# A block of seventeen residual stages in one kernel: the gated linear attention (Hgrn) stage between its projection products, cross attention in pairs of heads, and a finer wait before the down projections

## The reference

```
def gla_chunk(q, k, v, log_f, chunk):
    gc = jnp.cumsum(blocks(log_f), axis=3)
    g_last = gc[:, :, :, -1]
    q_dec = q * jnp.exp(gc)
    k_inv = k * jnp.exp(-gc)
    k_end = k * jnp.exp(g_last[:, :, :, None] - gc)
    att = jnp.where(causal, jnp.einsum('bnhlk,bnhsk->bnhls', q_dec, k_inv), 0.0)
    o_intra = jnp.einsum('bnhls,bnhsv->bnhlv', att, v)
    def step(state, inp):
        qd, ke, vv, gl = inp
        o = jnp.einsum('bhlk,bhkv->bhlv', qd, state)
        state = state * jnp.exp(gl)[..., None] + jnp.einsum('bhsk,bhsv->bhkv', ke, vv)
        return state, o
...
def hgrn2_mixer(h, in_w, lower_bound, norm_w, out_w):
    q, f, i, g = jnp.split(h @ in_w, 4, axis=-1)
    forget = lb + (1.0 - lb) * jax.nn.sigmoid(f.astype(jnp.float32))
    o = gla_chunk(heads(jax.nn.silu(q)) * H_EXPAND ** -0.5, heads(1.0 - forget), heads(i),
                  heads(jnp.log(forget)), HGRN_CHUNK)
    o = rmsnorm_2(o.astype(h.dtype), norm_w) * jax.nn.silu(heads(g))
    return o.reshape(bsz, seq, D_MODEL) @ out_w
...
def memory_cross_attention(h, mem_n, wq, wkv, wo):
    s = jnp.einsum('blhd,bmhd->bhlm', q, k).astype(jnp.float32) * X_HEAD_DIM ** -0.5
    p = jax.nn.softmax(s, axis=-1).astype(h.dtype)
    o = jnp.einsum('bhlm,bmhd->blhd', p, v).reshape(bsz, seq, D_MODEL)
    return o @ wo
```

## Time and profile before

| | us |
|---|---|
| median of 3 runs | 4009.58 |
| lowest and highest run | 3997.74, 4010.38 |
| the profiled execution | 4006.53 |
| span of its instructions | 4004.8 |
| TensorE matmul busy | 3823.6 |
| VectorE busy | 1061.4 |
| ScalarE busy | 721.6 |
| mean granted TensorE clock | 0.982 of full speed |

### The profile page before, as it was taken

The page is one execution under the profiler, slowest core; times in us unless marked ns, Lnnn a source line. Parts: engine busy times, 40 slices in busy tenths (PEclk is TensorE's granted clock), DMA queues, the critical chain, the costliest instruction groups (busy, mean ns, idle before and its releaser), DMA issues.

```text
span 4004.8 us, 37903 instructions
## 1 busy us (share of the span) xinstructions
PE 3823.6 (95%) x16756; PEld 2747.2 (69%) x16756; DVE 1061.4 (27%) x2069; ACT 721.6 (18%) x1361; POOL 16.4 (0%) x43
## 2 busy tenths in 40 slices
PE   6999999999999999999995899999999999999998
PEld 5856785875587775778564568667666877757684
DVE  5434341502410243112103202126420212431120
ACT  1004200001510242111001111023221102521110
POOL 1000000000000000000000000000000000000000
PEclk9999999999999999999996899999899999999999
DMA  9752584744234423334440124332222434333342
GB/s 374 283 199 107 212 300 176 276 147 147 107 145 154 153 106 126 131 130 160 147 147 21 65 105 168 141 135 103 106 107 105 153 142 154 119 121 132 132 154 88
DMA packets 42451, 598.45 MB, mean 149 GB/s; under 512 B 4736, under 2 KB 4752, under 8 KB 6192
## 3 DMA queue, kind: packets, MB, share of 16 engines
q1 hardware_dynamic: 41024, 589.94, 40.0%
q0 software_dynamic: 1264, 6.10, 0.4%
HBM read 594.97 MB, written 1.05 MB: 149 GB/s over the span
## 4 chain that ended last, share of the span: by engine, by line
PE 92%; DVE 5%; ACT 2%; issue 1%; DMA 0%; DVEq 0%
PE ps L449 33%; PE ps L328 12%; PE ps L345 9%; PE ps L1906 4%; PE ps L2202 3%; PE ps L361 3%; PE ps L2221 3%; PE ps L1939 2%; PE ps L1414 2%; PE ps L1064 1%; PE ps L1409 1%; PE ps L1434 1%; PE ps L474 1%; PE ps L645 1%; PE ps L371 1%
## 5 line engine op out<-in xcount | busy, mean ns | idle before, releaser
L449 PE MATMUL ps<-hT,ring 128*128 128x256 f32 (+1 forms) x7360 | 1327.7, 343 | 3.6 <-DVE stat L309 3.6
L449 PEld LDWEIGHTS ps<-hT,ring 128*128 128x128 f32 x7360 | 1194.9, 191 | 134.2 <-issue 7.7
L328 PE MATMUL ps<-ring,aT 128*128 128x512 f32 x1088 | 477.4, 600 | 20.1 <-DVE aT L2326 14.5
L328 PEld LDWEIGHTS ps<-ring,aT 128*128 128x128 f32 x1088 | 208.2, 193 | 280.2 <-issue 257.3
L345 PE MATMUL ps<-ring,aT 128*128 128x512 f32 x848 | 371.1, 595 | 9.0 <-ACT aT L2266 7.8
L345 PEld LDWEIGHTS ps<-ring,aT 128*128 128x128 f32 x848 | 160.1, 191 | 205.4 <-issue 194.4
L208 DVE SCALAR_TENSOR_TENSOR memT<-big,silu_c,memT 128x512 f32<-128x512 f32 x238 | 179.0, 752 | 8.5
L1906 PE MATMUL ps<-hT,ring 128*128 128x256 f32 x768 | 173.1, 382 | 0.0
L383 ACT ACTIVATE big<-x 128x1024 f32<-128x1024 f32 x34 | 35.9, 1057 | 759.5 <-DVE x L426 432.5
L1906 PEld LDWEIGHTS ps<-hT,ring 128*128 128x128 f32 x768 | 145.5, 191 | 26.1 <-issue 7.7
L426 DVE TENSOR_TENSOR x<-x,ps 128x1024 f32<-128x1024 f32 x22 | 26.9, 1221 | 432.1 <-PE ps L345 432.1
(11 more groups left out here) (481 smaller groups left out, 3450.0 us busy)
## 6 DMA issues: line engine op xcount, KB each, us to landing
ring<-weights_in SPq DMA_DIRECT2D x244, 2048.0 KB, 7.7
big<-ada_in SPq DMA_DIRECT2D x34, 2048.0 KB, 7.7
ring<-ada_in SPq DMA_DIRECT2D x2, 2048.0 KB, 27.4
big<-b_gate_in POOLq DMA_DIRECT2D x1, 1536.0 KB, 15.1
x<-x_in SPq DMA_DIRECT2D x1, 1024.0 KB, 5.0
big<-b_gate_in POOLq DMA_DIRECT2D x1, 1024.0 KB, 9.0
big<-mem_in POOLq DMA_DIRECT2D x1, 1024.0 KB, 5.3
out<-big SPq DMA_DIRECT2D x2, 512.0 KB, 2.6
```

The source lines that it names most:

```text
L328: last = pe.matmul(ps[:, 2 * t + half, :], aT[:, 4 * j + k, t * P:(t + 1) * P], w[:, k, half * 512:(half + 1) * 512], start=(4 * j + k == ...
L449: last = pe.matmul(ps[:, bank + m // 2, (m % 2) * SEQ + at:(m % 2) * SEQ + at + n], w[:, k, m * P:(m + 1) * P], hT[:, k, at:at + n], start ...
```

## The change

1. **Hgrn.** The pieces now come in the order f, f, q, i, q, i, g, g. The mixer works in two halves of four heads. Its products are no longer behind the last piece but at 48 numbered slots between the products of the last six pieces (`hgrn_fill_pe`). The intra-chunk products are full 128x128 products, 8 for a half (`hgrn_inside_pe`), where each chunk had its own; the states start from the first update and there are 7 updates and 7 state products for a half. The last half's transposes are inside the down projection (`down_halves_pe`, which is the former `down_attn_pe` with its waits and its transpose function as arguments). The making of the keys is moved to a function of its own (`down_keys_pe`). The constants of the scan go to `gdn_work`.
2. **Cross attention.** Scores, softmax, transposes and products are made for two pairs of heads. The second pair's scores and both pairs' transposes are between the products of v. The down projection waits for the first pair's tiles only, and for the second pair's before its second piece.
3. **Down projections of the gated stages.** `down_pe` and `last_pe` wait at first for the tenth piece's tiles, and for the eleventh's (`then`) ahead of their own last piece.

```
+        def hgrn_inside_pe(pe, half):
+            pe.wait_ge(hgrn_dve_done, HGRN_DVE[f"masked{half}"])
+            pe.wait_ge(hgrn_act_done, HGRN_ACT[f"v{half}"])
+            for t in range(TT):
+                for h in range(4):
+                    last = pe.matmul(ps[:, t, h * P:(h + 1) * P], hgrn_scores(half)[:, h, t, :], hgrn_tokens(6144, half)[:, t, h * P:(h + 1) * P], start=(h == 0), stop=False, skip_group_check=True)
+        def hgrn_update_pe(pe, half, c):
+            t, j = c // 4, c % 4
+            if c >= 2:
+                pe.wait_ge(hgrn_dve_done, HGRN_DVE[f"state{half}{c - 1}"])
+            for h in range(4):
+                at = 512 * half + h * P
+                last = pe.matmul(ps[:, 2 + c % 2, h * P:(h + 1) * P], view(big, 14336, TT, D)[32 * j:32 * j + 32, t, at:at + P],
+                                 view(big, 6144, TT, D)[32 * j:32 * j + 32, t, at:at + P], start=True, stop=True)
+        def hgrn_inter_pe(pe, half, c):
+            t, j = c // 4, c % 4
+            pe.wait_ge(hgrn_dve_done, HGRN_DVE[f"state{half}{c}"])
+            for h in range(4):
+                last = pe.matmul(ps[32 * j:32 * j + 32, t, h * P:(h + 1) * P], hgrn_part(0, half)[:, h, 32 * c:32 * c + 32], hgrn_state(c)[:, h, :], start=False, stop=True, skip_group_check=True)
+        def hgrn_fill_pe(pe, slot):
+            if slot == 8:
+                hgrn_ends_pe(pe, 0)
+            if slot == 11:
+                hgrn_scores_pe(pe, 0)
+            if slot == 13:
+                hgrn_ends_pe(pe, 1)
+            if slot == 27:
+                hgrn_scores_pe(pe, 1)
+            for half in range(2):
+                c = slot - 17 - 16 * half
+                if c == 0:
+                    hgrn_inside_pe(pe, half)
+                if 0 <= c < 7:
+                    hgrn_update_pe(pe, half, c)
+                if 0 < c < 8:
+                    hgrn_inter_pe(pe, half, c)
+            if slot == 45:
+                hgrn_turn_pe(pe, 0)
+        def hgrn_pe(pe, i, c0):
             first_channels_pe(pe, i, c0)
+            freed = ("f0", "f1", "q0", "v0", "q1", "v1")
+            for c in range(6):
+                pe.wait_ge(hgrn_act_done, HGRN_ACT[freed[c]])
...
+                            if k % 4 == 0:
+                                hgrn_fill_pe(pe, 8 * c + 2 * m + k // 4)
...
+                            if k % 2 == 0:
+                                hgrn_fill_pe(pe, 8 * c + 4 * t + k // 2)
...
+        def hgrn_act(act, c0):
+            act.wait_ge(hgrn_dve_done, HGRN_DVE["shifted"])
             act.activation(small[:, 8:40], small[:, 8:40], ACT.Exp).then_inc(hgrn_act_done, 1)
+            hgrn_chunk_act(act, c0, 0, hgrn_part(2048, 0), ACT.Sigmoid)
+            hgrn_chunk_act(act, c0, 1, hgrn_part(2048, 1), ACT.Sigmoid)
+            for half in range(2):
+                act.wait_ge(hgrn_dve_done, HGRN_DVE[f"forget{half}"])
+                act.activation(hgrn_flat(12288, half), hgrn_flat(2048, half), ACT.Ln).then_inc(hgrn_act_done, 1)
+            for half in range(2):
+                act.wait_ge(hgrn_dve_done, HGRN_DVE[f"sum{half}"])
+                act.activation(hgrn_flat(12288, half), hgrn_flat(10240, half), ACT.Exp).then_inc(hgrn_act_done, 1)
+
+                act.wait_ge(hgrn_dve_done, HGRN_DVE[f"gap{half}"])
+                act.activation(hgrn_flat(14336, half), hgrn_flat(14336, half), ACT.Exp).then_inc(hgrn_act_done, 1)
+                act.activation(hgrn_flat(8192, half), hgrn_flat(10240, half), ACT.Exp, scale=-1.0).then_inc(hgrn_act_done, 1)
+            hgrn_chunk_act(act, c0, 2, hgrn_part(0, 0), ACT.Silu)
+            for half in range(2):
+                act.wait_ge(hgrn_pe_done, HGRN_PE[f"ends{half}"])
+                act.wait_ge(hgrn_dve_done, HGRN_DVE["end1"])
+                act.copy(hgrn_tokens(14336, half), ps[:, 0:2, :]).then_inc(hgrn_act_done, 1)
+            hgrn_chunk_act(act, c0, 3, hgrn_tokens(6144, 0), ACT.Copy)
+            hgrn_chunk_act(act, c0, 4, hgrn_part(0, 1), ACT.Silu)
+            hgrn_out_act(act, 0)
+            hgrn_chunk_act(act, c0, 5, hgrn_tokens(6144, 1), ACT.Copy)
+            hgrn_root_act(act, 0)
...
+            hgrn_query_dve(dve, 0)
+            hgrn_masked_dve(dve, 0)
+            hgrn_states_dve(dve, 0, 1, 8)
+            hgrn_query_dve(dve, 1)
+            hgrn_masked_dve(dve, 1)
+            hgrn_norm_dve(dve, 0)
+            hgrn_states_dve(dve, 1, 1, 8)
+            hgrn_gate_dve(dve, 0)
+            hgrn_tiles_dve(dve, 0)
+            hgrn_norm_dve(dve, 1)
+            hgrn_gate_dve(dve, 1)
+            hgrn_tiles_dve(dve, 1)
```

Cross attention and the waits:

```
+            xattn_scores_pe(pe, n, 0)
+            for j in range(2):
+                pe.wait_ge(xattn_act_done, 8 * n + j + 1)
+                w = arrived(pe, c0 + 2 + j).rearrange("p (k c) -> p k c", k=KT)
                 for t in range(TT):
+                    if (j, t) == (0, 1):
+                        xattn_scores_pe(pe, n, 1)
+                    if (j, t) == (1, 1):
+                        xattn_turn_pe(pe, n, 0)
                     for k in range(KT):
+                        if (j, t, k) == (1, 1, 4):
+                            xattn_turn_pe(pe, n, 1)
...
+            xattn_values_pe(pe, n, 0)
+            xattn_values_pe(pe, n, 1)
...
             for t in range(TT):
                 for c in range(nc - 2, nc):
+                    if then and (t, c) == (0, nc - 1):
+                        pe.wait_ge(*then)
...
-            down_pe(pe, 0, (swiglu_dve_done, 11), c0=11, nk=22, ada=range(14, 18))
+            down_pe(pe, 0, (swiglu_dve_done, 10), c0=11, nk=22, ada=range(14, 18), then=(swiglu_dve_done, 11))
...
-            down_pe(pe, 7, (xattn_act_done, 7), c0=108, nk=8)
+            down_pe(pe, 7, (xattn_act_done, 8), c0=108, nk=8, then=(xattn_dve_done, 10))
...
-            down_pe(pe, 8, (convglu_dve_done, 44), c0=121, nk=22)
-            hgrn_pe(pe, 0, 8, c0=127)
-            down_pe(pe, 9, (hgrn_dve_done, 34), c0=135, nk=8, kc0=137, ki=1)
+            down_pe(pe, 8, (convglu_dve_done, 40), c0=121, nk=22, then=(convglu_dve_done, 44))
+            hgrn_pe(pe, 8, c0=127)
+            down_halves_pe(pe, 9, 135, [[(hgrn_act_done, HGRN_ACT["tiles0"]), (hgrn_dve_done, HGRN_DVE["tiles0"])], [(hgrn_act_done, HGRN_ACT["tiles1"]), (hgrn_dve_done, HGRN_DVE["tiles1"])]], hgrn_turn_pe, ())
+            down_keys_pe(pe, 9, 137, 1)
```

More of the change, by code:

```diff
@@ L309, in norm_dve, with down_pe @@
             dve.memset(stat[:, 63:64], 0.0).then_inc(norm_dve_done, 1)
[L311 removed]
+        def down_pe(pe, i, before, c0, nk, ada=(), kc0=None, ki=0, late=None, then=None):
             nc = -(-nk // 4)
@@ new lines, in xattn_values_pe @@
+        def xattn_values_pe(pe, n, pair):
+            if pair:
+                pe.wait_ge(xattn_act_done, 8 * n + 7)
+                pe.wait_ge(xattn_dve_done, 10 * n + 9)
+            else:
+                pe.wait_ge(xattn_act_done, 8 * n + 6)
+            v_tm, pT = view(big, 4096, TT, D), view(aTf, 2048, 8, SEQ)
+            for c in range(4 * pair, 4 * pair + 4):
+                for m in range(TT):
+                    last = pe.matmul(psf[:, 2048 + c * SEQ:2048 + (c + 1) * SEQ], v_tm[:, m, c * P:(c + 1) * P], pT[:, TT * (c // 2) + m, :],
+                                     start=(m == 0), stop=(m == 1))
+            last.then_inc(xattn_pe_done, 1)
@@ new lines, in hgrn_flat, with hgrn_tokens, hgrn_scores, hgrn_state @@
+        def hgrn_flat(start, half):
+            return view(big, start + 1024 * half, 1024)
+        def hgrn_tokens(start, half):
+            return view(big, start, TT, D)[:, :, 512 * half:512 * half + 512]
+        def hgrn_scores(half):
+            return view(aTf, 2048 + 1024 * half, 4, TT, P)
+        def hgrn_state(c):
+            return view(aTf, 4096 + 512 * (c % 2), 4, P)
+        def hgrn_ends_pe(pe, half):
+            pe.wait_ge(hgrn_dve_done, HGRN_DVE[f"end{half}"])
+            if half:
+                pe.wait_ge(hgrn_act_done, HGRN_ACT["ends0"])
+            for t in range(TT):
+                for h in range(4):
+                    last = pe.transpose(ps[:, t, h * P:(h + 1) * P], hgrn_part(2048, half)[:, h, t * P:(t + 1) * P], ident[:, :])
+            last.then_inc(hgrn_pe_done, 1)
@@ new lines, in hgrn_states_dve @@
+        def hgrn_states_dve(dve, half, first, last):
+            for c in range(first, last):
+                dve.wait_ge(hgrn_pe_done, HGRN_PE[f"update{half}{c - 1}"])
+                if c >= 3:
+                    dve.wait_ge(hgrn_pe_done, HGRN_PE[f"inter{half}{c - 2}"])
+                if c == 1:
+                    dve.tensor_copy(hgrn_state(1).rearrange("p h c -> p (h c)"), ps[:, 2, :]).then_inc(hgrn_dve_done, 1)
+                else:
+                    dve.wait_ge(hgrn_dve_done, HGRN_DVE[f"state{half}{c - 1}"])
+                    for h in range(4):
+                        at = 64 + 32 * half + 8 * h + c - 1
```

(10 more changed lines are left out.)

470 lines of the change are left out of this document (206 added, 264 removed), and 7 rows, old and new, of tables (HGRN_DVE, HGRN_PE).

## The result

The changed kernel takes 3839.9 us (median of 4 runs, 3835.2 to 3849.2) and the kernel before, on the same chip, 4007.3. The ratio is 0.9594, with a 95% interval of 0.9567 to 0.962. In a second group of runs on one chip it was 3843.7 against 4013.3, ratio 0.9583 (0.957 to 0.9596).

What follows compares the result with a forecast made beforehand. TensorE, busy for 95% of the span, was taken to bound the kernel. From 4006.5 us, 102.7 (Hgrn), 22.6 (cross attention) and 29.8 (gated stages) go, leaving 3851.4; with 1 us guessed for thin waits, 3852, range 3840 to 3872.

Steps and rivals of the forecast that it cites:

- What bounds the kernel: Whole kernel: TensorE, busy for 95% of the span; only less work or less standing still on it shortens the time.
- What goes in Hgrn: Hgrn: the whole stretch from the eighth piece's end to the down projection goes, 141.6 us.
- the 320 instructions at 0.109 us: Hgrn: the mixer work still on TensorE, placed between the pieces, 34.9 us in all.
- The changes of shape: Hgrn's slots 17 to 40: 44 changes of tile shape at 0.09 us, 4.0 us, with ends of 0 and 9.7.
- The row of the attention: Trace row used to price shape changes: 1.91 us where 1.73 is due, 0.18 for one in and one out.
- The side by side: Hgrn's updates: running tiles of one mode in parallel would not help, as each update uses one chunk's rows only.
- The chain beside the pieces: Hgrn's VectorE and ScalarE work: nothing late, decayed q at T+17.6 for scores at T+19.9, slack 2.3 us.
- the thin slots: Hgrn's slots 17 and 33, needing v: 0.5 us to spare each; narrowly met waits given 1 us as a guess.
- the state steps: Hgrn: a step of 1.26 us under 3.5 us of other work, covered; 17.6 us if the cover were gone.
- Cross attention and the finer waits: Four cross attention stages lose 22.6 us of waits; down projections of the gated stages lose 29.8 us.
- the fills that are not free: Rival in Hgrn: shape changes at 0.22 us each (+5.7 us) or state steps losing cover; 3858 to 3870, chance 0.12.
- the third rival: Small waits come back elsewhere: 52.4 us not gained, 3904 at most, or 3875 if half returns; chance 0.04.

Runs made afterwards that it cites:

- experiment 1: Changed kernel with the down projections of the gated stages waiting for the eleventh piece's tiles again, as before; 3883.1 us, ratio to before 0.9676.
- experiment 2: Changed kernel with the cross attention of before, all four heads at once; 3864.4 us, ratio to before 0.9635.
- experiment 3: Kernel before with the Hgrn part of the change alone; 3901.9 us, ratio to before 0.9723.
- experiment 5: Changed kernel with Hgrn's updates and state products on the full array, output not the reference's; 3838.4 us, Hgrn's distance 166.39 us against 173.57.
- second trace of before: Kernel before run once more, unchanged, for its trace; 3992.4 us.
- experiments 6 and 7: Changed kernel with two updates in one slot, two state products in the next: Hgrn's distance 167.25 us; then those updates also woven: 164.56 us, kernel 3832.6 us.

## Why the prediction was right, and its 12 us

**What bounds the kernel**: right, and time taken off TensorE came off the end; the traces of experiments 1 to 3 show each part by itself. By the two pages, 117 us of it were idle time and 54 us busy time. Of the busy time about 14 us are the 128 instructions less (an estimate, 128 x 0.109) and 10 the shorter solve. The rest is not divided by any run; the old Hgrn's instructions ran in a stretch with a mean clock of 0.70, and the new one's run at 1.00.

**What goes in Hgrn, and the 320 instructions at 0.109 us**: right for the traced execution; in the second trace of before the stretch that goes is 5.0 us shorter. Experiment 5 has the stage with no changes of shape at 3.51 us a slot, where 3.47 were counted.

**The changes of shape**: the mechanism is right and the size was too small, 0.16 us each by experiment 5 (7.2 us) for 0.09 (4.0 us), inside the ends of 0 and 0.22. The row of the attention was read wrongly. Its 0.18 us was halved as "a change in and one out", but from start to start a group of instructions holds one change (experiment 5: 0.20 for the projection products), and 44 x 0.18 = 7.9 us would have been near the 7.2. A cost of the other change can hide there, since the 64-row products of two heads overlap. The first four of them, of 256 columns, take 404.56 - 404.03 = 0.53 us, where one after another 4 x 0.216 = 0.86 would be due:

```profile
404.03 0.71 PE L1250 MATMUL ps<-big 64*128 64x256 f32 x4
404.56 0.39 PE L1251 MATMUL ps<-big 64*128 64x128 f32 x4
```

By the Trainium skill (TensorEngine Tiling (Array Packing), Key Properties) a change of mode drains the engine. Experiment 5 agrees that a change costs time, 0.16 us; it doesn't show what the engine does in it.

**The side by side that "would not help here"**: true of the change as it stands, with one chunk in a slot, but experiments 6 and 7 show that this was a choice of the order. So the lower bound of 0 for the changes of shape ("a gain is excluded") was wrong for the method: of the 173.57 - 164.56 = 9.0 us that experiments 6 and 7 gained, some 7 are the overlap (an estimate: 12 changes fewer at 0.16 are 1.9). The Trainium skill (TensorEngine Tiling (Array Packing), Key Properties) says that different tiles can work in parallel. The woven updates agree: 16 instructions in the time of 8, 1.09 us for 1.08.

**The chain beside the pieces, the thin slots, the state steps**: right to 0.1 us (T + 17.7 for 17.6), no wait at slot 17 or 33, and a cover of 4.0 us for steps of 1.1. The 1 us guessed for them was not there. The full products between fills take 1.93 us, within the 1.73 + 0.3 set as a sign of being wrong. The DMA share there is 0.28 (window of 2002 to 2126 us), just under the 0.3 to 0.4 expected.

**Cross attention and the finer waits**: the mechanism is right, and this term was mis-sized by reading a wait as its listed idle. The idle begins after the latency of the last product, so each wait is some 0.2 us more from start to start: 6.61 us for a cross attention with four waits listed as 5.66, 1.6 to 1.7 for a swiglu wait listed as 1.41. With the slower spell behind it, 1.6 to 1.8 us where 1.2 was read, a convolution wait is 6.7 us and not 6.0 (experiment 1). Together the marks show 61.6 us for 52.4; 1.7 of that is the lower clock in the second cross attention.

**The step that failed** is the one that set the sum against a single execution as if unchanged stages kept their length. Of the 17 us between the forecast's difference and that of the two traces, 10.8 are clock in stages that the change does not touch, and the other 6.4 are the terms above and the guess of 1 us. The allowance of "a few us between executions" was too small, although the runs of before lay 12 us apart. That the time came within 12 us of the forecast is in part luck, since the terms' errors have opposite signs: Hgrn gave 3.8 us less than forecast, the waits 9.2 us more. By the medians the kernel before loses more to the clock than the one traced: 4013.1 to 4013.3 us in three later groups of nine runs, with mean granted clocks of 0.973 to 0.981, where the traced one has 4006.5 and 0.982. Its Hgrn stretch varies with the clock, by 5.0 us between its two traces; the changed kernel's has no stop and had the same length in every trace with the same Hgrn. How the rest of the medians' difference divides is not shown: the later runs of before have no trace.

Of the rivals, the fills that are not free was the one with some truth, 3.2 us of its 5.7. None of the others happened. (In the third rival, half of 52.4 us makes 3878 and not 3875; nothing rested on it.)

## What to carry to other kernels

Put the small serial work of a stage between the large products of the same stage, with the slot numbers counted from the durations of the chain: here a step of up to 2.4 us cost nothing, with 4.0 us of other work between the product that feeds it and the one that needs it. When small products use a part of the array, do those of one shape together, and let neighbours use different rows of it, where the waits allow. And measure a change of under one part in a hundred by distances between marks in the trace, since at full clock these agree to 0.05 us, where the two traced executions of the kernel before differ by 14.

## What the runs showed of the hardware

- Changing from a 128x128 product to a 32-row one, to a 32-column one and back cost 0.16 us a change on average (44 changes, 7.2 us).
- Sixteen fp32 matmul instructions of 32 rows and 128 columns took 1.09 us when neighbouring products used different rows (and different PSUM banks), 1.64 when eight on the one rows came before eight on the other, and eight alone 1.08, each with one change of shape.
- Behind a stop of only 1.1 us, the granted clock went to 1.2 GHz for some 20 us in eight of twelve traces, in the same code. It did so while TensorE was never idle afterwards, in products of 64 rows and columns. In all eight it had also been at 1.2 GHz for a short while 29 us before, behind a stop of 1.7 to 1.9 us; it had been there in only one of the other four. Without the stop of 1.1 us it did not fall, in one trace and by their times in four more runs. Whether the small products alone can bring it down was not tried.
